# Norm and input projection of a diffusion block: two programs made one, tokens loaded first, the first unit's products in step with the fills

## The reference, cut to what matters

```python
mod_x = jax.nn.silu(c) @ w_mod[i] + b_mod[i]          # c (1024), w_mod 1024 x 6144
mod_c = jax.nn.silu(c_ctx) @ w_mod[i] + b_mod[i]
sh1, sc1, g1, sh2, sc2, g2 = jnp.split(mod_x[:, None, :], 6, axis=-1)
hx = _modulate(_rmsnorm(x, norm1_g[i]), sh1, sc1)      # x: 1024 tokens x 1024
hc = _modulate(_rmsnorm(ctx, norm1_g[i]), csh1, csc1)  # ctx: 256 tokens x 1024
zx = hx @ w_in[i] + b_in[i]                            # w_in 1024 x 5120
kvc = hc @ w_in[i][:, COL_K:COL_G_HY] + b_in[i][COL_K:COL_G_HY]
```

## Time and profile before

| | us |
|---|---|
| median of 3 runs (lowest, highest) | 2998.2 (2995.26, 3002.37) |
| the profiled execution: its time | 2996.65 |
| its span, first to last instruction | 2994.6 |
| PE busy | 2762.0 (92%) |
| DVE busy | 2233.8 (75%) |
| ACT busy | 1547.7 (52%) |
| DMA | 814.89 MB, mean 272 GB/s |

### The profile page before, as it was taken

The page is one execution under the profiler, slowest core; times in us unless marked ns, Lnnn a source line. Parts: engine busy times, 40 slices in busy tenths (PEclk is TensorE's granted clock), DMA queues, the critical chain, the costliest instruction groups (busy, mean ns, idle before and its releaser), DMA issues.

```text
span 2994.6 us, 35524 instructions
## 1 busy us (share of the span) xinstructions
PE 2762.0 (92%) x13697; PEld 2257.9 (75%) x13697; DVE 2233.8 (75%) x2214; ACT 1547.7 (52%) x1577; POOL 130.9 (4%) x147
## 2 busy tenths in 40 slices
PE   7899979888999977987599999999999999999997
PEld 2677878775767766876488888888888888888885
DVE  4575156643897893465888888888888898888987
ACT  4422146642212202022577777777777777777774
POOL 0010000000000010000000000000000000000000
PEclk8899988889999988998799999999999999999999
DMA  6698453223554576344699999999999999999995
GB/s 217 202 317 285 162 99 56 60 105 97 164 187 149 192 254 216 112 184 163 270 357 387 391 379 363 377 386 390 379 369 375 391 387 375 369 379 387 384 374 195
DMA packets 205460, 814.89 MB, mean 272 GB/s; under 512 B 31935, under 2 KB 93735, under 8 KB 126912
## 3 DMA queue, kind: packets, MB, share of 16 engines
q1 hardware_dynamic: 185618, 693.32, 61.9%
q0 software_dynamic: 19696, 119.56, 12.1%
HBM read 745.43 MB, written 67.39 MB: 271 GB/s over the span
## 4 chain that ended last, share of the span: by engine, by line
PE 48%; ACT 1%; issue 1%; DVE 1%; DVEq 0%; ACTq 0%
PE moe_ps_gate L1972 16%; PE moe_ps_up L1972 15%; PE moe_ps_y L1962 15%; PE moe_ps_h L1943 1%; ACT moe_w_hi L2013 1%; PE moe_ps_x L1935 0%; DVE raw L2135 0%; ACT moe_xt_hi L2006 0%; DVE moe_w_lo L2065 0%; DVE moe_h L2086 0%; ACT moe_sl L2026 0%; DVE raw L2122 0%; PE moe_ps_gate L1996 0%; PE moe_ps_gate L1998 0%; PE moe_ps_up L1996 0%
## 5 line engine op out<-in xcount | busy, mean ns | idle before, releaser
L2065 DVE TENSOR_TENSOR moe_w_lo<-raw,moe_w_hi 128x2048 fp32r<-128x2048 f32 x528 | 1207.4, 2290 | 159.8 <-ACT moe_w_hi L2013 159.3
L2013 ACT ACTIVATE moe_w_hi<-raw 128x2048 fp32r<-128x2048 f32 x528 | 1010.9, 1919 | 379.2 <-PE moe_ps_gate L1972 128.1
L1972 PE MATMUL moe_ps_up<-moe_w_hi,moe_xt_hi 128*128 128x512 f32 (+1 forms) x768 | 292.4, 381 | 0.0
L1972 PE MATMUL moe_ps_gate<-moe_w_hi,moe_xt_hi 128*128 128x512 f32 (+1 forms) x768 | 289.1, 376 | 1.4 <-DVE moe_xt_lo L2056 1.4
L1972 PE MATMUL moe_ps_gate<-moe_w_hi,moe_xt_lo 128*128 128x512 f32 (+1 forms) x768 | 286.4, 373 | 0.0
L1972 PE MATMUL moe_ps_up<-moe_w_hi,moe_xt_lo 128*128 128x512 f32 (+1 forms) x768 | 286.4, 373 | 0.0
L1972 PE MATMUL moe_ps_up<-moe_w_lo,moe_xt_hi 128*128 128x512 f32 (+1 forms) x768 | 285.9, 372 | 0.0
L1972 PE MATMUL moe_ps_gate<-moe_w_lo,moe_xt_hi 128*128 128x512 f32 (+1 forms) x768 | 285.9, 372 | 0.0
L1186 PE MATMUL hyena_ps_g<-hyena_h_parts,hyena_g_parts 128*128 128x256 f32 x1536 | 216.2, 301 | 37.1 <-DMA hyena_g_parts<-gw_d 23.7
L1186 PEld LDWEIGHTS hyena_ps_g<-hyena_h_parts,hyena_g_parts 128*128 128x128 f32 x1536 | 202.2, 203 | 47.7 <-DMA hyena_g_parts<-gw_d 25.7
L1962 PE MATMUL moe_ps_y<-moe_w_hi,moe_ht_hi 128*128 128x512 f32 x704 | 218.7, 392 | 0.0
(11 more groups left out here) (277 smaller groups left out, 4295.9 us busy)
## 6 DMA issues: line engine op xcount, KB each, us to landing
raw<-in_w_moe SPq DMA_DIRECT2D x528, 1024.0 KB, 7.4
hyena_g_parts<-gw_d POOLq DMA_DIRECT2D x64, 1024.0 KB, 5.7
proj_w_mod<-in_w_mod SPq DMA_DIRECT2D x32, 512.0 KB, 6.2
gw_d<-proj_g_parts POOLq DMA_DIRECT2D x16, 1024.0 KB, 7.4
w_in<-in_w_in SPq DMA_DIRECT2D x12, 1024.0 KB, 8.8
norm_w_mod<-in_w_mod SPq DMA_DIRECT2D x4, 2048.0 KB, 12.8
proj_g_raw<-in_w_in SPq DMA_DIRECT2D x16, 512.0 KB, 9.7
hyena_h_parts<-hq_d POOLq DMA_DIRECT2D x4, 2048.0 KB, 8.1
```

Source lines behind the costliest of these rows:

```text
L1972: mm = pe.matmul(ps, hp[:, e % 2, k, :], wp[:, r, :], start=(k == 0 and x == 0), stop=(k == KD - 1 and x == 2))
L2013: act.activation(w_hi[:, g % PARTS], raw[:, g % RAW], ACT.Copy).then_inc(hi_ready, 1)
L2065: dve.tensor_tensor(w_lo[:, g % PARTS], raw[:, g % RAW], w_hi[:, g % PARTS].bitcast(F32), ALU.subtract).then_inc(lo_ready, 1)
```

## The change

The two programs become one, `norm_and_project`.

- **Loads.** SP issues seven small loads and then the tokens; the other seven small ones go out on ACT's queue. The four `w_mod` chunks follow as 16 pieces of 0.5 MB in four buffers, each waiting for the use of its buffer (`piece_used`); unit 0 of `w_in` stands behind the eighth piece, unit 1 behind the last.
- **Order of the fills.** `fills` runs over all `k` of the first 512 tokens, then of the second 512, then of the context. PE turns the tokens of fill n + 2, waits for `lo_done` of fill n and makes the six products of unit 0 that read fill n. The eight context fills are turned inside unit 1 (`turn_ctx`, two fills at a time, into the bank of `ps_col`). ACT and DVE split unit 0 before the fills and unit 1 among them.
- **Order on DVE.** The second sine argument now stands behind the first four scaled token tiles, and the rows of `w_mod` between them.
- **Gate blocks.** They move two units later (`BLOCKS_AT` = 2), because their buffers lie where `x_raw` was: SP waits for all 24 turns (`xt_done`) before it loads them, and all that SP has behind that in its order waits too.
- The barrier between the programs is gone.

```diff
         groups = [(0, 4, 0), (4, 4, 0), (8, 2, 1)]
-        fills = [(k, g) for k in range(KD) for g in range(3)]
+        fills = [(k, g) for g in range(3) for k in range(KD)]
+        CTX_FILL = 2 * KD
+        uses = [4] * (SEG_HY[1] + SEG_Q[1]) + [5] * SEG_K[1]
+        first_use = [sum(uses[:u]) for u in range(len(uses) + 1)]
+        V_AT = first_use[-1]
+        BLOCKS_AT = 2
+
+        def blocks(u):
+            b = 2 * (u - BLOCKS_AT)
+            return range(b, b + 2) if 0 <= b < N_BLOCKS else range(0)
...
+        def bank(u, c, th):
+            return first_use[u] + (2 * th + c if u == 0 else 2 * c + th)
...
+                def load_piece(n, q):
+                    if n:
+                        sp.wait_ge(piece_used, PIECES * (n - 1) + q + 1)
+                    sp.dma_start(w_early[:, q], mod_src[n, q]).then_inc(w_mod_in[q], 16)
...
+                for t in range(0, TT, 4):
+                    sp.dma_start(x_raw[:, t:t + 4, :], x_src[:, t:t + 4, :]).then_inc(x_in[t // 4], 16)
+                sp.dma_start(x_raw[:, TT:NT, :], ctx_src).then_inc(x_in[2], 16)
                 for n in range(NC):
-                    if n >= 2:
...
-                for u in range(2):
-                    sp.dma_start(keep["w_in"][:, u], a["w_in"].rearrange("(k p) (u n) -> u p k n", p=P, n=UNIT)[u]
-                                 ).then_inc(keep["w_in_sems"][u], 16)
+                        load(0)
+                load(1)
                 sp.wait_ge(mlp_sin, 2)
                 sp.dma_start(a["hidden_d"], hidden[:]).then_inc(keep["kept"], KEPT_HIDDEN)
-                sp.wait_ge(keep["kept"], KEPT_HIDDEN)
+                sp.wait_ge(cols_ready, 4)
+                load_mod(0, 0)
+                load_mod(0, 1)
+                for u in range(SEG_V[0]):
...
+                    if u == BLOCKS_AT - 1:
+                        sp.wait_ge(xt_done, len(fills))
+                        load_b_mod(0)
+                        load_block(0)
+                        load_block(1)
+                        sp.dma_start(bv_rows[:], bass.AP(a["b_in"].tensor, 5 * 512, [[0, P], [1, 512]])).then_inc(bv_in, 16)
...
+                def turn(n):
+                    k, g = fills[n]
+                    t0, nt, _ = groups[g]
+                    if n >= 3:
+                        pe.wait_ge(full_ready, n - 2)
+                    for t in range(nt):
+                        mm = pe.transpose(ps_x[:, n % 3, t * P:(t + 1) * P], x_raw[:, t0 + t, k * P:(k + 1) * P], ident[:])
+                    mm.then_inc(xt_done, 1)
...
+                def turn_ctx(n):
+                    pe.wait_ge(full_ready, n)
+                    for x in range(2):
+                        k, t0 = fills[n + x][0], groups[2][0]
+                        for t in range(2):
+                            mm = pe.transpose(ps_col[:, (2 * x + t) * P:(2 * x + t + 1) * P],
+                                              x_raw[:, t0 + t, k * P:(k + 1) * P], ident[:])
+                    mm.then_inc(xt_done, 2)
...
+                def latent_step(u, c, k, halves):
+                    s = u % 2
...
+                            mm = pe.matmul(ps[:, bank(u, c, th) % BANKS, :], w, h[:, k, th * 512:(th + 1) * 512],
+                                           start=(k == 0 and first), stop=(k == KD - 1 and last))
+                            if k == KD - 1 and last:
+                                mm.then_inc(z_done, 1)
+
+                def latents(u):
+                    for c in range(CH_UNIT):
+                        bank_free(bank(u, c, 1))
+                        for k in range(KD):
+                            if u == 1 and k % 4 == 3:
+                                turn_ctx(CTX_FILL + 4 * c + k // 4 * 2)
+                            latent_step(u, c, k, range(2))
...
                 for n in range(NC):
-                    pe.wait_ge(w_in[n % 2], 16 * (n // 2) + 16)
                     if n >= 2:
                         pe.wait_ge(mod_row_ready, n - 1)
-                    for k in range(KD):
-                        mm = pe.matmul(ps_mod[0:2, n % 2, :], c_silu[:, k, :], w_mod[:, n % 2, k, :],
-                                       start=(k == 0), stop=(k == KD - 1))
-                    mm.then_inc(mod_done, 1)
-                    if n == 1:
+                    for q in range(PIECES):
+                        pe.wait_ge(w_mod_in[q], 16 * n + 16)
+                        for r in range(2):
+                            k = 2 * q + r
+                            mm = pe.matmul(ps_early[0:2, n % 2, :], c_silu[:, k, :], w_early[:, q, r, :],
+                                           start=(k == 0), stop=(k == KD - 1))
...
+                turn(0)
+                turn(1)
+                pe.wait_ge(lo_ready, 1)
+                for n in range(CTX_FILL):
+                    if n + 2 < CTX_FILL:
+                        turn(n + 2)
+                    k, th = fills[n]
+                    pe.wait_ge(lo_done, n + 1)
+                    for c in range(CH_UNIT):
+                        latent_step(0, c, k, (th,))
+                for u in range(1, SEG_V[0]):
+                    pe.wait_ge(lo_ready, u + 1)
...
+                split(0)
+                act.wait_ge(cols_ready, 4)
+                for n in range(CTX_FILL):
+                    fill(n)
+                    if n == 3:
+                        split(1)
+                for th in range(2):
+                    for c in range(CH_UNIT):
+                        evacuate_hy(0, c, th)
+                for u in range(1, SEG_V[0]):
+                    split(u + 1)
...
+                sine_argument(0)
+                dve.wait_ge(stats_done, NT)
+                dve.tensor_scalar(var[:], ss[:], 1.0 / D, EPS, ALU.mult, ALU.add).then_inc(var_ready, 1)
+                inverse_root(dve, dt, lambda: dve.wait_ge(stats_done, NT + 1), var[:], root[:], inv[:], tmp[:])
+                for t in range(4):
+                    normed(t)
+                early_row(0)
+                sine_argument(1)
+                early_row(1)
...
+                for t in range(4, NT):
+                    normed(t)
+                early_row(2)
...
+                dve.wait_ge(mlp_sin, 2)
                 split(0)
-                for u in range(SEG_V[0]):
+                early_row(3)
...
+                for n in range(CTX_FILL):
+                    low(n)
+                    if n == 4:
+                        split(1)
+                for c in range(CH_UNIT):
+                    convolve(0, c)
+                dve.wait_ge(keep["kept"], KEPT_HIDDEN)
```

More of the change, by code:

```diff
@@ L519, in _ @@
                     if u >= SEG_K[0]:
+                        pe.wait_ge(lo_done, len(fills))
                         context(u)
@@ new lines, in _ @@
+                act.wait_ge(var_ready, 1)
+                act.activation(root[:], var[:], ACT.Sqrt).then_inc(stats_done, 1)
+                act.wait_ge(mlp_arg, 2)
+                act.activation(hidden[:], arg[:], ACT.Sin).then_inc(mlp_sin, 1)
+                split(0)
+                act.wait_ge(cols_ready, 4)
[3 more added lines that the diff above has]
+                        split(1)
+                for th in range(2):
+                    for c in range(CH_UNIT):
+                        evacuate_hy(0, c, th)
@@ L562, in _ @@
+                for u in range(1, SEG_V[0]):
                     split(u + 1)
+                    if u == SEG_Q[0]:
+                        act.wait_ge(lo_done, len(fills))
                     for c in range(CH_UNIT):
-                        if u < N_BLOCKS // 2:
-                            split_block(2 * u + c)
-                        n, ch = first_use[u] + 2 * c, CH_UNIT * u + c
+                        for b in blocks(u)[c:c + 1]:
+                            split_block(b)
+                        if u == 1:
+                            for n in range(CTX_FILL + 4 * c, CTX_FILL + 4 * c + 4):
+                                fill(n)
+                        ch = CH_UNIT * u + c
@@ new lines, in _ @@
+                dve.tensor_copy(shift_col[:], col[:, 0])
+                for j in range(2):
+                    ins = dve.scalar_tensor_tensor(out=scale_col[:, j, :], in0=col[:, 1, j, :], scalar=1.0,
+                                                   in1=par[:, C_NORM1:C_BIN], op0=ALU.add, op1=ALU.mult)
+                ins.then_inc(cols_ready, 1)
+                dt.inc(dve.memset(z_pad[:, :, 0:1], 0.0))
+                dt.inc(dve.memset(z_pad[:, :, T + 1:T + 2], 0.0))
+                dt.wait()
@@ L656, in _ @@
                     for c in range(CH_UNIT):
-                        if u < N_BLOCKS // 2:
-                            split_block(2 * u + c)
+                        for b in blocks(u)[c:c + 1]:
+                            split_block(b)
+                        if u == 1:
+                            for x in range(CTX_FILL + 4 * c, CTX_FILL + 4 * c + 4):
+                                low(x)
                         if u < SEG_Q[0]:
@@ L671, in _ @@
```

(1 more changed line is left out.)

454 lines of the change are left out of this document (198 added, 256 removed).

## The result

The changed kernel takes 2971.7 us (median of 4 runs, 2966.5 to 2974.05), the kernel before in the same session 3000.28: ratio 0.9909, interval 0.9897 to 0.9922. The profiled execution took 2972.26 us, its span is 2970.2, the mean granted clock 0.964. The forecast was 2973 (2967 to 2984).

The account below looks back on a forecast made before the run. It took DMA, then ACT during the fills, then PE from the first product as the bound. 26.8 us gained less 1.7 lost gave 25, profiled time 2971.6, median 2973 us, range 2967 to 2984.

Parts of the forecast that it names:

- The fills with unit 0: Opening, fills merged with unit 0: 31.3 us from first product, unit 0 ending at 89.0 instead of 115.79, 26.8 us gained.
- The 2.5 us for slow clock and late split: Unit 0: low clock at its start and unit 1's splits delaying fill 5, together 2.5 us (bounds 0 and 4).
- The met waits: Unit 0: two already met semaphore waits a step, 0 to 4 us in all, taken as 1.
- The sums: PE's modulation sums: start at 20.3, no wait for pieces, end at 52.6 against 54.41, 1.8 us gained.
- Cover on DVE and ACT: Opening: squares, norm, sines and modulation rows all hidden behind PE's sums, by 1.5 to 2.5 us.
- Context turns: Unit 1: four groups of four transposes among products on PE, 0.43 us each, 1.7 us lost.
- SP's wait: End of unit 1: loads queued behind SP's wait for all turns cause no PE wait, by 6 us or more.
- late folds: Rival: late pieces and DVE's backlog stop PE at unit 2's end by 2 to 10 us; 2975 to 2983, chance 7%.
- Unchanged, almost one for one: Stages behind the opening follow unchanged, so its gain or loss should appear at the kernel's end almost one for one.
- The 25 us of the sum: Whole kernel: 26.8 us gained by unit 0's end less 1.7 lost in unit 1, 25 us.
- Clock stays low: Rival: PE's clock stays low through unit 0, which ends at 114; kernel about 2998 us, chance 6%.
- Pieces starve the sums: Rival: `w_mod` pieces land in 12.3 us, three rounds of 7.2 us, 21.6 lost in the sums; 2995, chance 4%.

Follow-up runs that it names:

- turns_first: Against the changed kernel, PE turns all sixteen latent fills before unit 0's first product; 2988.19 us, ratio 0.9974.
- w_lo_at_old_place: Against the changed kernel, four small tiles lie behind `w_lo`, so it begins at byte 132192 as in the kernel before; 2971.73 us, ratio 0.9914.

## Why the prediction was right, and where it was not

- **The fills with unit 0: right.** Forecast 31.3 us, measured 29.08. Products: 96 x 0.228 = 21.9 (21.8 forecast). Turns: a step is 64.07 - 62.27 = 1.80 us, less six products 0.44. The prediction counted 14 groups of turns among the products; there are 13, since three of the sixteen stand ahead of the first product, so they cost 5.7 us (6.0 forecast). The 2.5 us for slow clock and late split measured 29.08 - 21.9 - 5.7 = 1.5: the clock was 1.00 from the start, and the split of unit 1 made two products late, by 0.2 us (68.27 - 67.70 = 0.57, elsewhere 0.35) and 1.0 (71.07 - 69.74 = 1.33). The met waits, taken at 1 us, cost nothing that shows.
- **The sums: a term mis-sized by 3.3 us.** They ended at 55.9, not 52.6. The first began 1.9 us late (tokens landed at 20.7, 18.8 forecast), PE idled 1.33 us before the third chunk, for which I had taken no wait (unit 0's `w_in`, 1 MB, stands ahead of its pieces in the queue), and the last half took 14.09 for 13.7; the first half took 0.3 less than its 18.6. So "1.8 us gained" was in fact 1.5 lost. With 2.2 saved in unit 0, unit 1 began at 89.85 for 89.0.
- **Cover on DVE and ACT: right.** The last row waited 4.10 us for PE. With the last sum 3.3 us earlier, as forecast, 0.8 would have been left of it; the prediction had 1.5 to 2.5, so all was hidden, but more narrowly.
- **Context turns, SP's wait, late folds: right.** Four transposes at 93.99, the next product at 94.35, 0.36 us and the slower step behind it; and no fold product of the units shows idle time ahead of it (135.88 and 159.18 above). The row of the last modulation sum on DVE, with its wait, and the context turn on PE:

```profile
55.91 0.68 DVE L586 TENSOR_TENSOR norm_mod_row<-norm_ps_mod,norm_mod_row 2x512 f32<-2x512 f32 x1 [4.10 <-PE norm_ps_mod L412]
```

```profile
93.99 0.60 PE L348 MATMUL norm_ps_col<-identity,norm_x_raw 128*128 128x128 f32 x4
94.35 0.48 PE L362 MATMUL proj_ps<-h_hi,proj_w_hi 128*128 128x512 f32 x1
```

- **"Unchanged, almost one for one": the step that failed**, though its errors nearly cancelled and the total stood. The projection's later units were 1.7% slower by the place of `w_lo` (3 us), which no row of before could show and the addresses of the two programs could only have hinted at. Attention was 6 us shorter, in both pairs of profiles. That its time goes with the clock is shown. That delaying it shortens it rests on one pair of profiles (7.7 us later, 3.2 shorter) and the two kernels' times (4.5 us apart, without overlap of their runs). Why the clock falls less for starts at 378 to 382, and in one of two starts near 407, stays open. The 25 us of the sum and the 24.4 of the profiles agree partly by luck: 25.9 - 1.7 - 3.0 + 6.2 and some -3 behind it.
- **Clock stays low: refuted.** In unit 0 four transposes stand between every six products and the granted clock is 1.00; in `turns_first`, with transposes alone, it is 0.61. The Trainium skill, TensorE: Matmul & The Clock Gate, Part 4, says that a transpose doesn't count as PE-busy the same way. The second stretch agrees, though PE was also idle there for a third of the time (busy 12.56 of 19 us), which no run tells apart; the first shows that here products between the transposes were enough.
- **Pieces starve the sums: refuted in size.** 1.33 us of waiting against 21.6. From 36 to 40 us, with the 0.5 MB pieces and unit 0's `w_in` in flight, the queue moved 366 GB/s:

```profile
36.00:40.00 4.00, 4.00 (x11) 0.76 (x9) 3.90 (x7) 0.00 (x0) 0.00 (x0) 1.00 1.04 366
```

The Trainium skill, DMA: Bandwidth & Descriptors, section Bandwidth, asks for at least 1 MiB a transfer; in this ring 1 MB did not help: it ended the sums 6.3 us later than the changed kernel's 0.5 MB and 2.1 later than `w_lo_at_old_place`; the kernels' times (ratios 0.9931, 0.9921 and 0.9914) go the same way within their intervals.

## What to carry to other kernels

A stretch in which one engine turns and waits for another's evictions is the place to put products of the next stage: here 12.6 us by moving them among the turns, and the clock comes with them. The order of loads is worth a look by stage: what is loaded first should be what the bounding engine asks for first, small inputs included (the first product came 5.6 us earlier by it; a gain in the kernel's time was not shown for it alone). A gain in an early stage has to be read at the start of each later stage, in two profiles at least: tile addresses moved 3 us here and the clock 6, in stages with not one instruction changed, as much as edits of this size bring.

## What the runs showed that I had not expected

- A product of 128x512 in fp32r costs 226.8 to 232.4 ns by where the low half of the weights lies in SBUF. All three kinds of products get longer, also the two that do not read `w_lo`: 229.9 to 231.6 ns for 226.7 to 227.0, by kind, from 125 to 270 us. Traffic has no part in it: in the value units of the changed kernel, with the DMA engines idle from 330 to 350 us, the step is 228.8 ns against 226.7 in before.
- Attention, with the same 1600 products in every kernel, takes 242.2 to 251.0 us; the mean granted clock goes from 0.93 to 0.88 with it, and PE's idle time does not change. Holding its loads back, so that it began 7.7 us later, cost 4.5.
- Four 0.5 MB loads issued between the two token loads did not delay the small loads (first PE work at 8.91 us; 8.02 to 9.48 in the profiles of kernels with all tokens first, 8.63 in the changed kernel's); issued ahead of the tokens they did (10.78).
